# A gated recurrence: its finest level taken from the forget gate, and low parts of weight tiles moved between two engines

## The reference, cut to what matters

```
f = lb + (1 - lb) * sigmoid(f_pre);  k = 1 - f;  q = silu(q_pre);  v = i_in
b = cumsum(log f)                                  # within a chunk
a[t, s] = sum_d q[t, d] k[s, d] exp(b[t, d] - b[s, d])      for s <= t
state   = exp(b_last) * state + sum_s k exp(b_last - b) v
o = (q exp(b)) @ state + a @ v
o = o * rsqrt(mean(o * o) + eps) * out_norm * silu(g_pre);  out = o @ w_out
```

## Time and profile before

| | |
|---|---|
| median of three runs | 2928.18 us (2926.64 to 2930.99) |
| the profiled execution | 2927.46 us |
| its span, first to last instruction | 2925.2 us |
| the recurrence, first product of step 0 to the last wait of PE | 1550.68 to 1661.63 us |
| one settled head in it | 13.86 us |

### The profile page before, as it was taken

One profiled execution on the slowest core, in us unless ns is written; L12 is line 12 of the kernel. 1 busy time (PEld: TensorE's weight loads), 2 busy tenths in 40 slices (PEclk: granted clock), 3 DMA queues, 4 the chain that ended last, 5 costly groups with the idle time before them and its releaser, 6 DMA issues.

```text
span 2925.2 us, 43270 instructions
## 1 busy us (share of the span) xinstructions
PE 2893.8 (99%) x15746; PEld 2581.3 (88%) x15746; DVE 2364.2 (81%) x4466; ACT 1194.7 (41%) x1928; POOL 1285.6 (44%) x764
## 2 busy tenths in 40 slices
PE   8999999999999999999999999999999999999998
PEld 7678999999998888888887788999999998888887
DVE  7537999999878888888356758999998978888887
ACT  6543334444433333333436543334444433333333
POOL 4133565334444444442348643664334444444441
PEclk9999999999999999999999999999999999999999
DMA  4122568999999999998321032669999999999995
GB/s 152 37 100 90 165 183 311 367 377 363 372 379 398 361 362 361 359 357 320 107 95 57 30 116 91 199 197 366 365 379 351 381 396 378 361 358 364 360 362 212
DMA packets 346146, 799.96 MB, mean 273 GB/s; under 512 B 27984, under 2 KB 192080, under 8 KB 345680
## 3 DMA queue, kind: packets, MB, share of 16 engines
q1 hardware_dynamic: 235200, 478.32, 47.2%
q0 software_dynamic: 73728, 268.47, 24.1%
q10 hardware_dynamic: 37008, 50.41, 4.7%
HBM read 694.33 MB, written 102.76 MB: 272 GB/s over the span
## 4 chain that ended last, share of the span: by engine, by line
PE 94%; POOL 2%; ACT 2%; DVE 1%; issue 0%; DMA 0%; DVEq 0%; SPq 0%; ACTq 0%
PE PS L1640 29%; PE PS L1642 29%; PE PS L1641 29%; PE PS L1861 3%; PE PS L1840 1%; POOL w_lo L612 1%; POOL arena L651 1%; PE PS L1770 1%; PE PS L1771 1%; PE PS L1817 1%; DVE resid L1114 1%; ACT arena L713 0%; ACT PS L976 0%; ACT PS L977 0%; PE PS L1805 0%
## 5 line engine op out<-in xcount | busy, mean ns | idle before, releaser
L700 ACT ACTIVATE w_hi<-w_raw 128x1024 fp32r<-128x1024 f32 x607 | 641.4, 1058 | 758.2 <-PE PS L1642 691.1
L1640 PE MATMUL PS<-x_hi,w_hi 128*128 128x384 f32 (+1 forms) x2564 | 897.5, 350 | 0.0
L1642 PE MATMUL PS<-x_hi,w_lo 128*128 128x384 f32 (+1 forms) x2564 | 886.3, 346 | 0.0
L1641 PE MATMUL PS<-x_lo,w_hi 128*128 128x384 f32 (+1 forms) x2564 | 885.2, 345 | 0.0
L1640 PE MATMUL PS<-w_hi,x_hi 128*128 128x512 f32 x1744 | 679.7, 390 | 1.7 <-POOL w_lo L612 0.9
L1642 PE MATMUL PS<-w_hi,x_lo 128*128 128x512 f32 x1744 | 678.6, 389 | 0.0
L1641 PE MATMUL PS<-w_lo,x_hi 128*128 128x512 f32 x1744 | 678.5, 389 | 0.0
L623 POOL DMA_INDIRECT arena<-in_v_t,arena x256 | 427.0, 1668 | 557.4 <-DVE resid L1412 527.5
L612 POOL TENSOR_TENSOR w_lo<-w_raw,w_hi 128x1024 fp32r<-128x1024 f32 x167 | 414.7, 2489 | 493.3 <-ACT w_hi L700 493.2
L1389 DVE TENSOR_TENSOR w_lo<-w_raw,w_hi 128x1024 fp32r<-128x1024 f32 x440 | 536.6, 1219 | 97.1 <-ACT w_hi L700 92.0
L623 POOL DMA_INDIRECT arena<-in_u_rows,arena x256 | 363.9, 1421 | 509.9 <-DVE arena L1396 455.6
(11 more groups left out here) (203 smaller groups left out, 2314.1 us busy)
## 6 DMA issues: line engine op xcount, KB each, us to landing
w_raw<-in_u_t SPq DMA_DIRECT2D x256, 512.0 KB
w_raw<-in_v_t SPq DMA_DIRECT2D x256, 512.0 KB
acts_dram<-arena ACTq DMA_DIRECT2D x256, 192.0 KB
gates_dram<-arena SPq DMA_DIRECT2D x24, 2048.0 KB
arena<-acts_dram SPq DMA_DIRECT2D x256, 192.0 KB
arena<-gates_dram SPq DMA_DIRECT2D x64, 768.0 KB
w_raw<-in_hg_t SPq DMA_DIRECT2D x40, 512.0 KB
w_raw<-in_pq_t SPq DMA_DIRECT2D x32, 512.0 KB
```

The costliest lines, as they stand in the source:

```text
L700: act.activation(w_hi[:, slot, :], w_raw[:, slot, :], ACT.Copy).then_inc(hi_ready, 1)
L1640: pe.matmul(ps, wh, xh, start=start, stop=False)
L1641: pe.matmul(ps, wh, xl, start=False, stop=False)
L1642: return pe.matmul(ps, wl, xh, start=False, stop=stop)
```

## The change

1. The finest level is no longer computed by differences and exponentials. For neighbours, exp(b[t] - b[s]) is the forget gate f[t] itself. So the keys are k itself and the queries f * q. To have the latter in one instruction, `gk` now holds f - 1, that is minus k; DVE copies it as keys and writes (gk + 1) * gq as queries, and the sign comes back in the output gain (-0.5 in place of 0.5). POOL makes seven differences per head, ACT seven exponentials; the products and masks stay.
2. Nine tiles have their low part made inside the recurrence. Six stay on POOL, at other steps; three (gate tiles 5 and 7, output tile 1) go to DVE, after step 3 of heads 2, 4 and 6.
3. In head 0, ACT copies the transposed key after step 3 and not after step 5.

```diff
 def low_by_dve(n):
+    if BASE["hg_q"] <= n < BASE["pq1"]:
+        return n in (BASE["hg_g"] + 5, BASE["hg_g"] + 7, BASE["hg_out"] + 1)
...
+            low_at = {8: ("hg_g", 2), 14: ("hg_g", 3), 20: ("hg_g", 4), 28: ("hg_g", 6), 40: ("hg_out", 0),
+                      56: ("hg_out", 2)}
             for n in range(8 * HEADS):
-                take_diff(n)
-                if n % 8 == 0 and n >= 16:
-                    head_roots(n // 8 - 2)
...
+                h, k = divmod(n, 8)
+                if k < LEVELS:
+                    take_diff(LEVELS * h + k)
+                if k == 0 and h >= 2:
+                    head_roots(h - 2)
+                if n in low_at:
+                    name, m = low_at[n]
+                    lows(BASE[name] + m, BASE[name] + m + 1)
...
-                    if 8 * h + k >= 2:
-                        level_exp(8 * h + k)
-                    if k == 5:
+                    if k < LEVELS and LEVELS * h + k >= 2:
+                        level_exp(LEVELS * h + k)
+                    if k == (5 if h else 3):
                         ready(act, ("kd", h))
...
-            chain(dve.tensor_scalar(out_gain, out_gain, 0.5 * P ** 0.5, None, ALU.mult))
+            chain(dve.tensor_scalar(out_gain, out_gain, -0.5 * P ** 0.5, None, ALU.mult))
...
-                chain(dve.tensor_scalar(gk[:, h, :], gb[:, h, :], -1.0, 1.0, ALU.mult, ALU.add))
+                chain(dve.tensor_scalar(gk[:, h, :], gb[:, h, :], 1.0, None, ALU.subtract))
...
+                if k == LEVELS:
+                    dve.tensor_copy(keys, level_keys(gk[:, h, :], m))
+                    dve.scalar_tensor_tensor(queries, level_queries(gk[:, h, :], m), 1.0,
+                                             level_queries(gq[:, h, :], m), ALU.add, ALU.mult)\
+                        .then_inc(sem("level_x"), 1)
+                    return
...
+                if k == 3 and h in (2, 4, 6):
+                    low(BASE["hg_g"] + 5 + (h - 2) if h < 6 else BASE["hg_out"] + 1)
```

More of the change, by code:

```diff
@@ L498, in scaling_used @@
         def scaling_used(eng, n):
-            if n >= 0 and n % 8 == 0:
-                eng.wait_ge(sem("k_decayed"), n // 8 + 1)
+            if n >= 0 and n % LEVELS == 0:
+                eng.wait_ge(sem("k_decayed"), n // LEVELS + 1)
             elif n >= 0:
-                eng.wait_ge(sem("level_x"), n // 8 * LEVELS + n % 8)
+                eng.wait_ge(sem("level_x"), n // LEVELS * LEVELS + n % LEVELS)
         def product_at(ap, c):
@@ L637, in take_diff @@
             def take_diff(n):
-                h, k = divmod(n, 8)
+                h, k = divmod(n, LEVELS)
                 if n >= 2:
@@ L1017, in _ @@
                              ("kd", h))
+                    if k == 5:
                         if h < HEADS - 1:
@@ L1108, in norm, with low @@
                          ("xT", k, c))
+            def low(n):
+                dve.wait_ge(hi_ready, n + 1)
+                dve.tensor_tensor(w_lo[:, n % RING, :], w_raw[:, n % RING, :], f32(w_hi[:, n % RING, :]),
+                                  ALU.subtract).then_inc(dve_low, 1)
             def add_to_resid(name, t):
@@ L1384, in make_onehots @@
                        .then_inc(onehots, 1)
[L1386 to L1390, removed]
                 def far_dot(k):
@@ L1485, in scale_level @@
                 h, k = divmod(n, 8)
-                d = scaling(n)
-                dve.wait_ge(sem("level_exp"), n + 1)
+                d = scaling(LEVELS * h + k)
+                if k < LEVELS:
+                    dve.wait_ge(sem("level_exp"), LEVELS * h + k + 1)
                 if k == 0:
```

## The result

The changed kernel takes 2937.76 us (median of eight runs, 2935.40 to 2939.59) where the one before takes 2928.18: a ratio of 1.0031, with a 95% interval of 1.0020 to 1.0042. It is slower by 9.6 us. The forecast of 2932.1 was 5.7 us too low, its range (2921.5 to 2939.0) holds the time, and the time lies nearer to the second rival (2936.9). The profiled execution took 2935.4 us with a span of 2933.5; before it was 2927.46 and 2925.2.

The account below looks back on a forecast made before the run. PE is busy nearly throughout, so only its waits count; PE and DVE close the settled loop. Gains -6.0, low parts ahead of step 5 +1.8, lock +7.0, low parts on DVE +1.1: +3.9, 2932.1 us, range 2921.5 to 2939.0.

Parts of the forecast that it names:

- the second rival: DVE's step 7 and query: POOL wins each time, product waits for a whole difference; 1.5 us per head, 2936.9, chance 0.25.
- What bounds the kernel: Recurrence: PE is busy nearly throughout, so only its waits count; in settled heads PE and DVE close the loop, not POOL.
- The lock: End of heads: DVE's copy, product and decayed query, reading SBUF, wait for POOL's differences; seven heads x 1.0 = 7.0 us.
- The settled head: Head 5, 13.86 us before, was to last 13.86 - 0.3 + 1.0 = 14.6 us.
- the sign of being wrong towards slower: Settled head 5 in the profile after: over 15 us would show the forecast wrong towards slower.
- the locks miss each other: Rival: DVE's three instructions at the head's end fall beside POOL's waits; -5.0 us, 2923.2, chance 0.27.
- nothing matters: Rival: POOL and ACT were not waited for, gains in heads 0 and 1 get eaten; 2928, no change, chance 0.03.
- The gains: Recurrence: PE waits ended in heads 0 and 1, late masks and levels, plus a cheaper copy; 6.0 us saved.
- 1.43 for head 0: Head 0: PE's wait for ACT's copy of the transposed key ends with the copy at step 3; 1.43 us saved.
- The low parts ahead of step 5: Heads 2 and 3: POOL's low part delays exponentials, key copy and PE's state products; 0.9 per head, 1.8 us lost.
- The low parts on DVE: Three 1.22 us low parts wait 0.40 for POOL's differences 4 to 6; 1.1 us lost (0 to 2).
- The copy's saving: Step 7: a one-operand copy of 0.21 to 0.41 us replaces a product; 0.1 per head, 0.8 us saved for eight.

Follow-up runs that it names:

- through PSUM: Changed kernel, but ACT copies both step 7 factors into PSUM and DVE's copy and product read them there: 2929.35 us, ratio 1.0001 against the kernel before.
- the late query: Changed kernel with the decayed query moved behind step 0 of the next head: 2932.46 us; with step 7's factors also in PSUM: 2924.94 us, ratio 0.9986.

## Why the prediction was right, and where not

- **What bounds the kernel.** Right: PE's busy time stayed, and the loss came mostly from PE's waits behind DVE (8.6 + 2.3 us, before 2.5 + 1.5), with about 1 us in head 2 behind ACT and about 1.5 from the clock, for which the prediction had no term. That POOL looks like the bound and isn't was right as well: it has 18 us less to do, and nothing came of it.
- **The lock.** Right in kind and place, and the copy with one operand waits like the others. The reason given for the meeting was only half of it: without the roots' low part the differences did slide onto DVE's step 7, but at the ends of heads 4 and 6 POOL still makes a low part, and there the copy waits for that (1.07 and 1.06 us; 0.71 to 1.04 in the heads where it meets a difference). The finest level alone, with every low part in its old place, lost more. So the operands from SBUF are enough. This term was the one most mis-sized: 7.0 us were put, 13.5 of waiting measured (1.9 per head over seven; 3.2 of the 13.5 the queries had before too, nearly all in heads 0 and 1). By head the copy was put at 0.40 and waited for 0.60, the query at 0.40 and waited for 0.47. The largest miss is the product's: 0.20, because it "follows the copy at once". It does, but POOL's queued difference goes in between, so that it waits for most of one: 0.86. That is the mechanism of the second rival, and 1.9 lies past the 1.5 us per head that it named. With 13.5 in place of 7.0 the sum is +10.4, and +9.6 was measured; that is near, but other terms missed too, and not every wait of DVE reached PE. So the forecast's place and the rival's price came true together. That the range held is partly luck: its end was worked out with 1.8 us per head, and with 1.9 and the same low-part terms it would be 2939.9, past 2939.0; the time stayed inside because those terms came out smaller.
- The Trainium skill ("SBUF — State Buffer", Who interferes with whom) calls the shared pair an exclusive lock. The trace agrees (1.26 us in place of 0.42, and 0.42 again through PSUM). The turns are read from this trace.
- **The settled head.** 14.6 us was forecast for head 5, and 14.69 measured; but head 5 is the one whose query ran free, so the match is partly luck. Heads 4 and 6 took 15.5, over the 15 that was named as the sign of being wrong towards slower.
- **The other rivals.** That the locks miss each other happened for one query of a settled head, head 5's; the copy and the product met POOL there as well. That nothing matters fell with the lock: undone, it gave back most of the loss.
- **The gains.** The waits at the state products of heads 0 and 1 went, as forecast. The sum without lock and without the copy's 0.8 would be -2.3. The version through PSUM gained nothing, with the query waiting 0.7 us more in all; with the late query as well it gained 4.4 (1.5 to 6.7 by the interval). Neither is a test of the 6.0 alone. What was wrong is to add up 1.43 for head 0 by itself: done alone it gave nothing by the middle of head 1, since the next wait there grew by more (1.24 to 3.00). Its gain needs the low parts of head 1 out of the way too.
- **The low parts ahead of step 5.** The waits came where they were forecast, 2.24 and 1.24 us. 1.8 us were put for the two. Head 3, which waits for 1.24, takes 15.62 us, head 4 without such a wait 15.48: a head is as long as its later chain, and DVE's was late anyway. Head 2, which waits for 2.24, takes 16.60 us, and 15.49 with its low part moved away. So about 1.2 us are borne out, nearly all in head 2; moving the low parts returned nothing because head 1 then paid. The 6.05 us that PE was said to need from there to step 7 were 6.2 in head 2: there are five eighths of the gate in that stretch and not four.
- **The low parts on DVE.** 1.22 + 0.40 was forecast, 1.64 to 1.65 us measured in heads 4 and 6 (1.75 in the mean of the three). The next scaling starts right at their end; their cost in time wasn't measured by itself.
- **The copy's saving.** Undisturbed it takes 0.29 us, near the middle of the 0.21 to 0.41 that was put. The estimate by the Trainium skill ("VectorE: DVE Perf Modes", the table of the errata), 0.19, is too low here.
- **The parts do not add.** Alone they moved the time by +12.5, +0.2 and +2.9 us against their kernels before; together by 9.6. The rows above show that each shifts the phase of POOL against DVE and that the waits change with it; that this is the whole reason wasn't tested.

## What to carry to other kernels

Before a factor of a DVE instruction is moved from PSUM to SBUF, look in the trace at what POOL does in that moment: beside a busy POOL each such instruction pays for most of one POOL instruction, and instructions in a row pay each time, because the two take turns. If another engine has time, let it put one operand into PSUM; here this gave back 8.9 of 9.6 us, though DVE's copy then takes 0.42 us in place of 0.29. And where two engines pass each other by 0.1 us there is no room: here, taking out a wait elsewhere made every turn of the loop from head 2 to head 6 slower.

## What was not expected of the hardware

- DVE and POOL alternate. At the end of a POOL instruction the waiting DVE instruction goes, at its end the waiting POOL one, also between two DVE instructions that follow each other with no gap (copy 1.07, product 1.26 us in head 4). It isn't so everywhere. Far ahead of the recurrence an instruction of DVE stood through two low parts, the last of five in a row that POOL made from 355.84 for 11.82 us (timeline of DVE, after):

```profile
362.63 5.12 DVE L1308 TENSOR_SCALAR arena<-arena 128x128 uint32<-128x128 uint32 x1
```

What sets this apart from the turns was not tried.
- POOL pays too, but less: three differences take 3.78 us against 3.11.
- A fall of TensorE's granted clock to 0.50 for 6 us behind a wait of 2.05 us cost about 1.5 us in head 7, where DVE came to wait for PE. A cost of this size doesn't show in the medians; the rows of the two traces show it.
